# Neighbourhood attention: the softmax scaling moved from VectorE to GpSimd, and the last bias tables made between the scalings

## What is computed

```python
def neighbourhood_attn(q, k, v, kc, vc, rpb):
    ...
        s_loc = jnp.einsum('bqhd,brqjhd->bhqrj', qr, kw) * scale + bias[None]
        s_ctx = jnp.einsum('bqhd,bchd->bhqc', qr, kc) * scale
        s = jnp.concatenate([s_ctx, s_loc.reshape(B, H, GRID_W, wr * NA_WIN_C)], axis=-1)
        p = jax.nn.softmax(s.astype(jnp.float32), axis=-1).astype(v.dtype)
        p_loc = p[..., Lc:].reshape(B, H, GRID_W, wr, NA_WIN_C)
        return (jnp.einsum('bhqc,bchd->bqhd', p[..., :Lc], vc)
                + jnp.einsum('bhqrj,brqjhd->bqhd', p_loc, vw))
```

## Time and profile before

| | |
|---|---|
| median of 3 runs | 4203.38 us (4201.72 to 4211.35) |
| time of the profiled execution | 4203.75 us |
| its span in the trace | 4202.0 us |
| mean granted TensorE clock over the span | 0.982 of 2.4 GHz |
| PE matmul busy | 3966.7 us (94%) |
| DVE busy | 1665.3 us (40%) |
| ACT busy | 1033.5 us (25%) |
| POOL busy | 827.7 us (20%) |
| units of layer 0, first `scores` to last `gather` start | 1675.57 to 1748.05 us |
| units of layer 1, first `scores` to last `gather` start | 3168.95 to 3224.00 us |

### The profile page before, as it was taken

How to read it: one execution, slowest core, us unless ns; L and a number is a source line. 1 busy time by engine, 2 the same in 40 slices (tenths; PEclk the granted TensorE clock), 3 DMA queues, 4 the chain that set the end, 5 groups by cost and what they waited for, 6 DMA issues and landing times. The chain is left out here.

```text
span 4202.0 us, 65040 instructions
## 1 busy us (share of the span) xinstructions
PE 3966.7 (94%) x28190; PEld 2682.4 (64%) x28190; DVE 1665.3 (40%) x2602; ACT 1033.5 (25%) x2159; POOL 827.7 (20%) x658
## 2 busy tenths in 40 slices
PE   8999999999999999998999799999899999979888
PEld 6788889887888766566555433333575778833332
DVE  2685854364445342637434300000435464421102
ACT  2212522222111221515211322111314252221111
POOL 2100022123442022212233101000122134400000
PEclk9999999999999999999999899999999999989999
DMA  3684300123223222010112399999320102389997
GB/s 113 212 282 148 91 17 4 45 101 111 81 81 102 68 62 84 10 61 1 60 61 100 138 374 388 387 389 376 106 93 27 61 21 101 121 350 427 426 427 308
DMA packets 196792, 673.84 MB, mean 160 GB/s; under 512 B 12174, under 2 KB 78414, under 8 KB 171678
## 3 DMA queue, kind: packets, MB, share of 16 engines
q1 hardware_dynamic: 190782, 649.76, 41.0%
q0 software_dynamic: 5728, 19.93, 1.6%
HBM read 647.50 MB, written 25.98 MB: 160 GB/s over the span
## 5 line engine op out<-in xcount | busy, mean ns | idle before, releaser
L559 PE MATMUL psum<-arena 128*128 128x264 f32 (+2 forms) x7120 | 1782.9, 412 | 14.5 <-DVE arena L627 6.5
L559 PEld LDWEIGHTS psum<-arena 128*128 128x128 f32 x7120 | 1348.8, 190 | 442.2 <-issue 11.6
L1458 PE MATMUL psum<-arena 128*64 128x512 f32 x3072 | 696.8, 600 | 43.6 <-DMA arena<-in_w_e 39.4
L1458 PEld LDWEIGHTS psum<-arena 128*64 128x64 f32 x3072 | 211.3, 137 | 466.4 <-issue 425.0
L594 ACT ACTIVATE arena<-psum 128x256 f32<-128x256 f32 (+2 forms) x405 | 169.8, 419 | 927.7 <-PE psum L559 869.5
L458 POOL TENSOR_TENSOR arena<-arena 128x512 f32<-128x512 f32 (+1 forms) x114 | 165.5, 1451 | 1020.4 <-PE psum L559 963.8
L2412 DVE TENSOR_TENSOR arena<-arena,psum 128x512 f32<-128x512 f32 x32 | 22.0, 687 | 788.6 <-PE psum L1466 534.2
L386 PE MATMUL psum<-arena 128*128 128x265 f32 (+2 forms) x1120 | 256.1, 386 | 3.3 <-ACT arena L3124 3.3
L386 PEld LDWEIGHTS psum<-arena 128*128 128x128 f32 (+1 forms) x1120 | 208.7, 188 | 43.0 <-ACT arena L3124 3.7
L2874 PE MATMUL psum<-arena 64*64 64x64 f32 x7424 | 225.8, 219 | 8.5 <-issue 4.5
L2874 PEld LDWEIGHTS psum<-arena 64*64 64x64 f32 x7424 | 223.9, 135 | 11.5 <-issue 8.7
(11 more groups left out here) (410 smaller groups left out, 3910.4 us busy)
## 6 DMA issues: line engine op xcount, KB each, us to landing
arena<-in_w_e SPq DMA_DIRECT2D x192, 2048.0 KB, 12.3
arena<-in_w_in SPq DMA_DIRECT2D x38, 2048.0 KB, 8.1
arena<-in_w_ada SPq DMA_DIRECT2D x24, 2048.0 KB, 8.4
arena<-in_ffn_up SPq DMA_DIRECT2D x22, 1024.0 KB, 7.5
arena<-in_w_branch SPq DMA_DIRECT2D x6, 2048.0 KB, 7.9
arena<-in_ffn_down SPq DMA_DIRECT2D x8, 1408.0 KB, 7.8
arena<-in_w_in SPq DMA_DIRECT2D x16, 512.0 KB, 4.5
arena<-in_w_out SPq DMA_DIRECT2D x4, 2048.0 KB, 8.5
```

The lines of the kernel that those rows point to most:

```text
L559: mm = pe.matmul(PS[:, bank, 0:cn], loaded, moved, start=fresh and k == 0, stop=k == h - 1, skip_group_check=not fresh)
L1458: mm = pe.matmul(PS[c * HD:c * HD + HD, b + (m > 0), :], x(kk), w[:, k, c * BW:c * BW + BW], start=(kk == 0), stop=(kk == KT - 1))
```

## The change

The two `tensor_scalar` of `normal(n)` leave DVE, which only makes the inverse sums and counts `na_r`. POOL waits for `na_r` and does the two scalings of each unit, written as two multiplications, the second by the constant 1.0. Of POOL's five table groups only (2, 0) is made first; the other four are made one by one after the scalings of units 0 to 3.

```diff
             wt(pool, "rpb_in", 16 * NA_H)
-            for g in range(4):
-                bias_of(nc.gpsimd, 2, g)
-            bias_of(nc.gpsimd, 1, 3)
+            late_tables = ((2, 1), (2, 2), (2, 3), (1, 3))
+            bias_of(nc.gpsimd, 2, 0)
+            for n in range(len(na)):
+                wt(pool, "na_r", n + 1)
+                for h in range(2):
+                    x = at(NA_S(n) + h * BW, CTX if na[n][1] else BW)
+                    inc(nc.gpsimd.tensor_scalar(x, x, at(cell(n, 2) + h, 1), 1.0, ALU.mult, ALU.mult), "na_p")
+                if n < len(late_tables):
+                    bias_of(nc.gpsimd, *late_tables[n])
             wt(pool, "na_o", len(na))
...
                 def normal(n):
                     wt(dve, "na_e", 2 * n + 2)
-                    step(V.reciprocal(at(cell(n, 2), 2), at(cell(n, 1), 2)))
-                    step.done()
-                    for h in range(2):
-                        x = at(NA_S(n) + h * BW, CTX if na[n][1] else BW)
-                        inc(V.tensor_scalar(x, x, at(cell(n, 2) + h, 1), None, ALU.mult), "na_p")
+                    inc(V.reciprocal(at(cell(n, 2), 2), at(cell(n, 1), 2)), "na_r")
```

## The result

The changed kernel takes 4227.07 us (median of 5 runs, 4221.73 to 4229.41) against 4209.18 us for the kernel before on the same chip (4201.72 to 4211.35): ratio 1.0045, 95% interval 1.0034 to 1.0055. It is slower, by 17.9 us where 9.7 had been forecast, and lies outside the predicted range (4210.5 to 4215.5). The forecast of 4213.0 was added to 4203.38, the median of three runs; the five runs of the kernel before have 4209.18, so 5.8 of the 14.1 us between forecast and result lie in the kernel before and not in the change. The profiled execution took 4227.82 us, its span 4225.9 us against 4202.0.

What follows compares the result with a forecast made beforehand. PE's own work and an equally long two-unit chain through DVE were taken to bound the units; +5.1 us (layer 1) and +4.6 (layer 0) made +9.7, added to 4203.38 for 4213.0 us, own range 4210.5 to 4215.5.

Steps and rivals of the forecast that it cites:

- The two-unit chain: Full units: turn, scores, bias addition, maxima, inverse, scaling, next turn; 6.23 us per two units, growing to 6.91.
- A + 3.22: Layer 1's full units: bias addition 3.22 us after A, the start of a unit's turn on PE.
- The end of each layer's units: Last inverse to last turn: POOL's way 1.81 us, stretched pair up to 0.7 us a layer; nothing counted.
- two such operations slow one another about twofold: End of units: read from a token sum of 3.04 us beside POOL's addition L450 of 2.67, alike at 1.26.
- Rival D: PE's clock drops with more idle time in the units, PE being 90% busy; given no chance of its own.
- The term of the hops: Two-unit steps between full units' turns: +0.68 us each; with starts, +5.1 in layer 1 and +4.6 in layer 0.
- The starts: First units of each layer: +0.5 us at turn 4 of layer 0, +0.3 at layer 1's start.
- A (POOL's preparation): Layer 0's first scaling: POOL's first tensor_scalar needs preparing, 3 us over the cover, total 4216; chance 0.28.
- B (the slow form): POOL's scalings: constant 1.0 brings the 1566 ns form, +2.32 us a hop, total 4236 to 4243; chance 0.08.
- C (not slower): POOL's pair short enough: no measurable change, 4207 at 1.11 us, or a gain down to 4197; chance 0.12.
- The tables cost nothing: Table groups between POOL's scalings: 1.49 + 1.15 = 2.64 us fits within 3.45 a unit, so no cost.
- It has no slack: Two-unit chain: any lengthening from inverse to turn comes back as time in every second unit.

Runs made afterwards that it cites:

- e1: The changed kernel with DVE's token sums behind the units waiting until POOL has scaled the last unit; 4214.60 us against 4207.60, ratio 1.0019.
- e2: The changed kernel with the last unit of each layer scaled by DVE instead of POOL; 4213.48 us against 4207.60, ratio 1.0015.
- e5: The changed kernel with each of the four token sums replaced by a one-input tensor_scalar of the same size; one run, 4224.68 us.
- e6: e2 with the inverse of unit n-1 moved ahead of the maxima of full unit n on DVE; 4204.84 us against 4208.66, ratio 0.9990.
- e8: The changed kernel with DVE scaling head 0 and POOL head 1, the last unit on DVE; 4208.36 us against 4208.66, ratio 0.9998.
- e3: The changed kernel with one multiplication in POOL's scaling, the constant 1.0 left out; 4259.92 us against 4207.60, ratio 1.0122.
- e9: e2 with all five table groups made by POOL ahead of its first scaling; one run, 4215.94 us.
- e7: The kernel before with inverse and both scalings of unit n-1, all on DVE, ahead of unit n's maxima; 4227.70 us against 4208.66, ratio 1.0045.

## Why the prediction was wrong

**The bound and the mechanism were right.** The two-unit chain has the places that were forecast, to 0.01 us: bias addition at A + 3.22, inverse at A + 5.10, hand-over 0.25 (0.26 forecast), end to turn 0.05 (0.06). PE now waits for POOL in every second full unit.

**The step that failed is "The end of each layer's units", with "I count nothing and keep 1.4 us for the range".** It measured +6.02 us in layer 0 and +6.42 in layer 1, 12.4 in all, and this alone carries the result out of the range: 4227.07 less 12.4 is 4214.7. (That this would be inside is in part luck: the kernel before came out 5.8 us higher than it had, the hops 3.6 lower than forecast.) Its ground was "two such operations slow one another about twofold", taken from one overlap. That row was misread. The line of the kernel before that stands just ahead of it:

```profile
1750.26 1.28 POOL L448 TENSOR_TENSOR arena<-arena 128x512 f32<-128x512 f32 x1
```

This addition, beside the same sum, took its usual 1.28 us, while the sum took 3.04 instead of 1.75, 1.29 more: as long as the addition. The next addition, L450, took 2.67 instead of 1.26 and ended 1.13 us behind the sum's end, almost a whole usual duration later. These times fit two engines that take turns, each held for about as long as the other ran, and not two that run at half speed. A ratio near two is what one such exchange happens to give. At the end of the units four sums follow each other without a gap, and POOL's pair was stretched 4.3 times (1.36 to 5.87 us), until the third had ended; DVE gave up only 0.4 us in two of its four sums (2.13 and 2.16 instead of 1.74). The prediction saw that the sums would start beside the last scaling. Its bound should have been the whole run of sums, four of 1.75 us, and not a ratio. e1 and e2 remove the overlap in two different ways and take 11.2 and 11.1 us off the stretches. They fall short of 12.4 by the start of layer 1: turn 2 stands 12.56 us behind the first scores in the changed kernel, 13.77 in e1 and 13.96 in e2, for a reason given below.

The Trainium skill (SBUF — State Buffer, "Who interferes with whom") says that a DVE instruction with two SBUF inputs contends with a GpSimd instruction that reads SBUF, and that in DVE's 2-port modes, which `tensor_scalar` can enter, the one that comes second is blocked for the whole instruction. The traces agree that both contend: the pair took 5.87 us beside two-operand sums and 3.47 beside one-operand `tensor_scalar` (e5), but 1.36 beside bias additions and beside maxima (e6), which read PSUM and no more than one operand in SBUF. They also show what that comes to for a run of instructions. In five places (both layers of the changed kernel, both of e5, and e8) a POOL scaling that found DVE at work ended 0.47 to 0.56 us behind the end of a DVE instruction, a little less than its usual 0.69. That POOL gets in only where one DVE instruction ends is read from these times; no run put a gap between the sums. Why the second scaling passed by the end of the second instruction, in all four pairs, stays open.

**The second half of that end, the clock, was not foreseen.** Rival D looked for a drop from a busy share of 90% and gave it no chance. Through the units that holds. It was asked of the wrong place: behind one wait of 4.64 us the granted clock over 7 us was 0.57, and turn 15 to the projection took 1.97 us longer, in each layer. With the wait gone (e1) the transposes take 1.06 again. e5 stands between: nothing was lost behind its wait of 1.82 us, 1.03 us behind that of 2.25.

**The term of the hops was too large, 9.7 forecast and 6.1 measured.** The pair is 1.36 us, not 1.49, so a hop costs 0.53, not 0.68. With the hops as counted this is exact: from turn 4 to turn 22 layer 0 went from 52.09 to 55.30 us, +3.2 = 6 x 0.53, and from turn 2 to turn 14 layer 1 went from 37.35 to 40.56, the same again. The starts make up the other half of the difference: turn 4 of layer 0 moved by +0.03 (+0.5 forecast), turn 2 of layer 1 by -0.32 (about +1 forecast). The latter is mostly chance and not the change: at this place the clock dips in some executions, in the kernel before but not in the changed one, and e1 and e2, which have the dip too, moved turn 2 by +0.89 and +1.08, as forecast. The best case of 768 ns for 512 elements that the prediction took from the Trainium skill (GPSIMD Engine Reference, "Elementwise — side-by-side cycle accounting") is above what was measured: one undisturbed scaling took 0.69 us.

Windows at the start of layer 1, for the kernel before:

```profile
3175.00:3182.00 7.00, 6.94 (x42) 4.02 (x43) 5.72 (x11) 5.01 (x11) 0.00 (x0) 0.76 0.04 16
```

and for the changed one:

```profile
3189.00:3196.00 7.00, 6.02 (x47) 3.94 (x48) 4.22 (x7) 4.94 (x12) 6.12 (x11) 1.00 0.02 6
```

The clock dips in the first turns of layer 1 before the change and not after it; it also dips in e1, e2, e3, e8 and e9, and not in e5, e6 and e7. The busy share ahead of it is alike (3.21 and 3.12 us of 7), so what decides it stays open. It makes about 1 us of one layer's stretch uncertain in every comparison here, e6's gain in layer 1 included.

**The rivals.** A (POOL's preparation) fell: the first scaling follows its inverse in 0.27 us. The Trainium skill (GPSIMD Engine Reference, "Instruction dispatch") has about 6 us for a first call; 2.54 us of idle POOL lay ahead of this one, and in e9 none did, and neither shows any such time. B (the slow form) fell for this change, and e3 shows that it is about one multiplication against two; in this place it would have cost 52 us, not 33. Of the 49.9 that its stretches show 11.9 are the ends, which that sum left out; it also counted 13 hops where the text has 14 elsewhere, and most of the rest lies in the first units, where a table follows each pair. C (not slower) fell. The tables cost nothing, as said: behind each of them the scaling still starts 0.25 to 0.28 us after its inverse. The later work gave nothing back, as said: from the units of layer 0 to those of layer 1 the two traces differ by 0.3 us.

**What "It has no slack" left out.** The prediction took DVE's order as given. e6 shows that the 1.2 us of maxima between the bias addition and the inverse were the slack: once the scaling is off DVE, the inverse can go first at a cost of 0.1 us for the maxima, and the longer way through POOL fits. This version is faster than the kernel before by 0.1% (interval 0.01% to 0.19%), which is 3.8 us by the medians and 2.8 by the stretches; only the 1.7 us of layer 0 are free of the dip in the clock.

## What to carry to other kernels

Work given to POOL has to be priced beside what DVE does at that very moment, and a run of SBUF-to-SBUF instructions on DVE without a gap can hold POOL for most of its length (here until the third of four had ended); look above all at the last item of a loop, where DVE is let go to the next phase. A PE wait of a few us may have to be priced a second time for the clock behind it: here 4.64 us cost another 1.97, 2.25 another 1.03, 1.82 nothing. When an operation leaves an engine, look at that engine's order again: the gain may lie in what can now go first.

## What was not expected of the hardware

- POOL's `tensor_scalar` on 128x512 f32 took 0.69 us with two multiplications and 1.56 with one (256 elements: 0.48 and 0.92).
- A pair of POOL scalings took 1.36 us alone, 5.87 beside back-to-back two-operand sums of DVE and 3.47 beside one-operand `tensor_scalar`; one scaling took 0.98 beside one of DVE's, instead of 0.69. DVE lost 0.4 us in two instructions of four, and nothing in its scaling. In all of these the held scaling ended about half a us behind the end of a DVE instruction.
- Behind a PE wait of 4.64 us transposes took 1.97 us instead of 1.09, at a granted clock of 0.57 over 7 us. Behind one of 1.82 us nothing was lost; behind one of 2.25 the transposes took 1.09 but the gathers after them ran at the lower clock, and 1.03 us were lost.
